# Four tiles of an output projection computed as two pairs of seven block products instead of eight

## The reference, cut to what matters

```python
m = sigmoid(proj[..., o5:o6]) * y_a + sigmoid(proj[..., o6:]) * y_b
x = x + gate * (m @ w_out[l])          # the output projection
...
return rms_norm(x, g_final), ...       # mean square over the 1024 channels of a token
```

## Time and profile before

| | |
|---|---|
| median of 3 runs | 940.15 us (938.82 to 940.74) |
| the profiled execution | 938.97 us, span of the trace 937.2 us |
| PE busy | 916.6 us, 98% of the span |
| DVE / ACT / POOL busy | 736.6 / 385.9 / 88.7 us |
| block products (26 pairs and 8 small ones) | from about 85 to 640.6 us of the span |
| output projection, tiles 1 to 5 | 844 to 901 us |

### The profile page before, as it was taken

One profiled execution on the slowest core, in us unless ns is written; L12 is line 12 of the kernel. 1 busy time (PEld: TensorE's weight loads), 2 busy tenths in 40 slices (PEclk: granted clock), 3 DMA queues, 4 the chain that ended last, 5 costly groups with the idle time before them and its releaser, 6 DMA issues.

```text
span 937.2 us, 16711 instructions
## 1 busy us (share of the span) xinstructions
PE 916.6 (98%) x6928; PEld 897.4 (96%) x6928; DVE 736.6 (79%) x862; ACT 385.9 (41%) x540; POOL 88.7 (9%) x97
## 2 busy tenths in 40 slices
PE   8999999999999999999999999999999999999996
PEld 5699999999999999999999999999999999999996
DVE  1797999997999996989995899999897642443346
ACT  5483355434453443453443454345535311112342
POOL 0121211111021011111010310000000000000000
PEclk9999999999999999999999999999999999999999
DMA  9978998889688989798798985449851524142105
GB/s 368 337 192 216 217 230 230 239 254 235 163 218 243 263 235 243 192 234 245 251 244 251 227 198 154 140 139 322 363 227 46 221 117 157 45 170 102 45 1 181
DMA packets 77741, 191.14 MB, mean 204 GB/s; under 512 B 11617, under 2 KB 18145, under 8 KB 73697
## 3 DMA queue, kind: packets, MB, share of 16 engines
q1 hardware_dynamic: 48176, 119.54, 36.5%
q0 software_dynamic: 19328, 46.17, 24.8%
q10 hardware_dynamic: 10160, 24.35, 7.3%
HBM read 164.07 MB, written 80.49 MB: 261 GB/s over the span
## 4 chain that ended last, share of the span: by engine, by line
PE 65%; DVE 26%; DMA 3%; issue 3%; ACT 1%; SPq 1%; DVEq 0%; ACTq 0%
DVE conv_y L1635 12%; PE ps L844 11%; PE ps L847 11%; PE ps L845 10%; PE ps L907 10%; PE ps L913 10%; PE ps L909 10%; DVE hr L1514 4%; DMA ada_raw<-w_ada 2%; DVE pool_s L1594 1%; DMA raw<-w_sums 1%; DVE bf L1708 1%; DVE stage_hi L1714 1%; DVE sig L1599 1%; DVE pool_p L1611 1%
## 5 line engine op out<-in xcount | busy, mean ns | idle before, releaser
L1635 DVE SCALAR_TENSOR_TENSOR conv_y<-conv_u,par_all,conv_y 128x1024 f32<-128x1024 f32 x240 | 300.6, 1278 | 2.1 <-DVE conv_y L1621 0.6
L907 PE MATMUL ps<-tr,hr 128*128 128x258 f32 x824 | 215.8, 283 | 5.2 <-DVEq L1582 3.4
L909 PE MATMUL ps<-tr,hr 128*128 128x258 f32 x824 | 216.3, 283 | 0.0
L1209 ACT ACTIVATE hr<-raw 128x512 fp32r<-128x512 f32 (+1 forms) x188 | 116.1, 619 | 140.0 <-PE ps L913 66.9
L913 PE MATMUL ps<-tr,hr 128*128 128x258 f32 x824 | 166.3, 283 | 0.0
L907 PEld LDWEIGHTS ps<-tr,hr 128*128 128x128 f32 x824 | 156.8, 190 | 6.1 <-issue 4.1
L907 PE MATMUL ps<-hr 128*128 128x258 f32 x616 | 160.9, 282 | 1.0 <-DVE pool_u L1539 1.0
L909 PE MATMUL ps<-hr 128*128 128x258 f32 x616 | 161.5, 283 | 0.0
L909 PEld LDWEIGHTS ps<-tr,hr 128*128 128x128 f32 x824 | 155.7, 189 | 0.0
L1514 DVE TENSOR_TENSOR hr<-raw,hr 128x512 fp32r<-128x512 f32 (+1 forms) x188 | 126.0, 673 | 8.1 <-ACT hr L1209 4.0
L913 PEld LDWEIGHTS ps<-tr,hr 128*128 128x128 f32 x824 | 127.2, 188 | 0.0
(11 more groups left out here) (200 smaller groups left out, 1276.2 us busy)
## 6 DMA issues: line engine op xcount, KB each, us to landing
w_sums<-w_main POOLq DMA_DIRECT2D x56, 512.0 KB, 9.0
raw<-w_sums SPq DMA_DIRECT2D x104, 256.0 KB, 4.0
raw<-w_main SPq DMA_DIRECT2D x82, 256.0 KB, 4.6
w_sums<-w_sums POOLq DMA_DIRECT2D x26, 512.0 KB, 5.6
w_raw<-w_main SPq DMA_DIRECT2D x24, 512.0 KB, 4.5
w_sums<-w_main ACTq DMA_DIRECT2D x22, 512.0 KB, 5.2
ada_raw<-w_ada SPq DMA_DIRECT2D x8, 1024.0 KB, 20.8
bf<-x_t SPq DMA_DIRECT2D x4, 1032.0 KB, 8.3
```

The lines of the kernel that those rows point to most:

```text
L907: nc.tensor.matmul(bank[:, c, :], wh[:, w_cols], x_hi[:, k, t_cols], start=start and k == 0, stop=False, skip_group_check=True)
L909: nc.tensor.matmul(bank[:, c, :], wh[:, w_cols], x_lo[:, k, t_cols], start=False, stop=False, skip_group_check=True)
L1209: nc.scalar.activation(ring(q)[0][:, 0:n], raw4[:, q % 4, 0:n], ACT.Copy).then_inc(item_hi, 1)
L1635: ins = v.scalar_tensor_tensor(out=y, in0=conv_u[:, x, k:k + SEQ], scalar=par_all[:, g, x, k:k + 1], in1=y, op0=ALU.mult, op1=ALU.add)
```

## The change

Tiles 0 and 1 of the output projection stay plain, tiles 2 and 3 and tiles 4 and 5 become two pairs (A and B) of seven block products, and tiles 6 and 7 stay chunk by chunk, now 7 ahead of 6. The four sums of blocks of m are made by DVE from the full rows of m, split by ACT and DVE, and lie in the rows that held a (the hidden rows of the convolution branch, `zone_h` and `zone_b`). The 14 weight blocks pass through a ring in `w_raw`, `w_hi` and `w_lo`. A fourteenth round of weight sums is added on POOL. x is no longer loaded at once into eight rows: it is loaded tile by tile into two rows (`x_res`), each load behind the tile that frees the row. In the diff `...` stands for what is left out.

```diff
...
+OUT_A, OUT_B = N, N + 1
+OUT_TILE = {OUT_A: 2, OUT_B: 4}
+OUT_ITEMS = [("P1", OUT_A), ("P1", OUT_B), ("P6", OUT_A), ("P2", OUT_A), ("P7", OUT_A), ("P5", OUT_A), ("P4", OUT_A), ("P3", OUT_A),
+             ("P6", OUT_B), ("P2", OUT_B), ("P7", OUT_B), ("P5", OUT_B), ("P4", OUT_B), ("P3", OUT_B)]
+OUT_AT = {item: i for i, item in enumerate(OUT_ITEMS)}
+FIRST_STRASSEN = JOB_OUT + 2
...
-MEAN_AT = {3 * 9 + 1: 0, 3 * 9 + 2: 1, 3 * 12 + 1: 2, 3 * 12 + 2: 3}
+MEAN_AT = {3 * 9 + 1: 0, 3 * 9 + 2: 1, 3 * 12 + 1: 2, 3 * 12 + 2: 3, 3 * 13 + 1: 4, 3 * 13 + 2: 5}
...
+        out_tr = [at("out_tr_h", [2, 2, KH, HALF], F32R, zone_h), at("out_tr_b", [2, 2, KH, HALF], F32R, zone_b)]
+        out_tf = [at("out_tf_h", [2, 2, KH, HALF], F32, zone_h), at("out_tf_b", [2, 2, KH, HALF], F32, zone_b)]
+        u2_out, u3_out = row_mean[:, 0:HALF], row_mean[:, HALF:TOK]
+        sq_tile = pool_s1[:, 0:TOK]
...
+        def x_res(m):
+            return stage_lo[:, m % 2, :] if m < KT - 2 else hf[:, m - (KT - 2), :]
...
+            if q >= OUT_SPLIT:
+                s, half = raw_slot(q) // 2, raw_slot(q) % 2
+                cols_ = slice(half * FORM_COLS, (half + 1) * FORM_COLS)
+                return w_hi[:, s, cols_], w_lo[:, s, cols_]
...
+            def load_out_item(i):
+                form, n = OUT_ITEMS[i]
+                if i < 4:
+                    sp.wait_ge(w_lo_done, lo_count(JOB_OUT + i // 2))
+                else:
+                    sp.wait_ge(item_lo, OUT_SPLIT + i - 3)
...
+            load_x(0)
+            load_x(1)
+            for i in range(4):
+                load_out_item(i)
+            sp.wait_ge(x_new_ready, 1)
+            load_x(2)
+            sp.wait_ge(x_new_ready, 2)
+            load_x(3)
+            for i in range(4, len(OUT_ITEMS)):
+                load_out_item(i)
+            sp.wait_ge(x_new_ready, 3)
+            load_x(5)
+            sp.wait_ge(x_new_ready, 4)
+            load_x(4)
+            sp.wait_ge(item_lo, OUT_SPLIT + 12)
+            sp.dma_start(w_raw[:, 1, :], t["w_main"][MAIN_B + JOBS - 1 - JOB_B]).then_inc(raw_full[1], 16)
+            sp.wait_ge(item_done, LAST + OUT_AT["P6", OUT_B] + 1)
+            load_x(6)
+            load_x(7)
+            sp.wait_ge(item_lo, OUT_SPLIT + 14)
+            sp.dma_start(w_raw[:, 0, :], t["w_main"][MAIN_B + JOBS - 2 - JOB_B]).then_inc(raw_full[0], 16)
...
+            for step in range(3 * SUM_CHUNKS + 3):
                 c, k = step // 3, step % 3
                 if c >= 1:
                     sum_phase(c - 1, 3 + k)
-                if c < N // 2:
+                if c < SUM_CHUNKS:
                     sum_phase(c, k)
                 if step in MEAN_AT:
                     add_row(MEAN_AT[step])
-            for r in range(4, 6):
-                add_row(r)
...
-            job_pairs(JOB_OUT + 1, 4, m_hi, m_lo)
-            single(JOB_OUT + 5, m_hi, m_lo)
+            single(JOB_OUT + 1, m_hi, m_lo)
+            def out_t_product(i, bank, form, n, start=False):
+                if n == OUT_A:
+                    pe.wait_ge(t_lo_done, 4 + OUT_T_LO.index(form) + 1)
+                block_product(OUT_SPLIT + i, bank, out_t(form, 0), out_t(form, 1), start=start).then_inc(item_done, 1)
+            for i, (form, n) in enumerate(OUT_ITEMS):
+                pe.wait_ge(item_lo, OUT_SPLIT + i + 1)
+                if form == "P1":
+                    pe.wait_ge(dve_evac, FIRST_STRASSEN - 1 + (n - OUT_A) - JOB_B)
+                    block_product(OUT_SPLIT + i, bank_a(n), gr[:, 0:KH, HALVES[0]], gr[:, KT:KT + KH, HALVES[0]], start=True).then_inc(item_done, 1)
+                if form == "P2":
+                    pe.wait_ge(seeded, n + 1)
+                    block_product(OUT_SPLIT + i, bank_b, gr[:, KH:KT, HALVES[0]], gr[:, KT + KH:2 * KT, HALVES[0]]).then_inc(item_done, 1)
+                if form == "P3":
+                    pe.wait_ge(c22_out, n + 1)
+                    block_product(OUT_SPLIT + i, bank_c, gr[:, KH:KT, HALVES[1]], gr[:, KT + KH:2 * KT, HALVES[1]]).then_inc(item_done, 1)
+                if form == "P6":
+                    pe.wait_ge(seeded, n + 1)
+                    out_t_product(i, bank_a(n), form, n)
+                if form == "P7":
+                    pe.wait_ge(u2_ready, n + 1)
+                    out_t_product(i, bank_a(n), form, n)
+                if form == "P4":
+                    pe.wait_ge(u3_ready, n + 1)
+                    out_t_product(i, bank_a(n), form, n)
+                if form == "P5":
+                    pe.wait_ge(c12_out, n)
+                    out_t_product(i, bank_c, form, n, start=True)
...
+                    if c == 0 and s == JOBS - 1 and k == 0:
+                        pe.wait_ge(w_lo_done, lo_count(FIRST_STRASSEN))
+                        pe.wait_ge(c21_out, OUT_B + 1)
+                        pe.wait_ge(c11_out, OUT_B + 1)
+                    if c == 0 and s == JOBS - 2 and k in (0, KH):
+                        pe.wait_ge(w_lo_done, lo_count(FIRST_STRASSEN + 1 + k // KH))
...
+            out_t_hi("P5", 1)
+            out_t_hi("P7", 2)
+            item_split(OUT_SPLIT)
+            item_split(OUT_SPLIT + 1)
+            out_t_hi("P6", 3)
+            out_t_hi("P4", 4)
+            tile_square(0, 0)
+            item_split(OUT_SPLIT + 2)
+            item_split(OUT_SPLIT + 3)
+            out_seed(OUT_A)
+            tile_square(1, 1)
+            for i, (form, n) in enumerate(OUT_ITEMS):
+                act.wait_ge(item_done, LAST + i + 1)
+                if form == "P6":
+                    if n == OUT_B:
+                        act.wait_ge(c12_out, n)
+                    nc.scalar.activation(halves(u2_out), bank_a(n), ACT.Copy).then_inc(u2_ready, 1)
+                if form == "P7":
+                    if n == OUT_B:
+                        act.wait_ge(c22_out, n)
+                    nc.scalar.activation(halves(u3_out), bank_a(n), ACT.Copy).then_inc(u3_ready, 1)
+                if (form, n) == ("P2", OUT_A):
+                    out_seed(OUT_B)
+                if i + 4 < len(OUT_ITEMS):
+                    item_split(OUT_SPLIT + i + 4)
...
+            def out_result(i):
+                form, n = OUT_ITEMS[i]
+                m = OUT_TILE[n]
+                landed = 16 * (m // 2 + 1)
+                first, second = HALVES
+                if form not in ("P2", "P5", "P4", "P3"):
+                    return
+                dve.wait_ge(item_done, LAST + i + 1)
+                if form == "P2":
+                    dve.wait_ge(xres_loaded[0], landed)
+                    v.scalar_tensor_tensor(out=halves(hf[:, KT + m, first]), in0=bank_b, scalar=mod[:, 4 + m // 4, m % 4, 0:1],
+                                           in1=halves(x_res(m)[:, first]), op0=ALU.mult, op1=ALU.add).then_inc(c11_out, 1)
+                if form == "P5":
+                    dve.wait_ge(u3_ready, n + 1)
+                    v.scalar_tensor_tensor(out=halves(hf[:, KT + m + 1, second]), in0=bank_c, scalar=-1.0, in1=halves(u3_out),
+                                           op0=ALU.mult, op1=ALU.subtract).then_inc(c22_out, 1)
+                    dve.wait_ge(c22_out, n + 1)
+                    dve.wait_ge(xres_loaded[1], landed)
+                    second_half(m + 1)
+                if form == "P4":
+                    link(v.scalar_tensor_tensor(out=halves(hf[:, KT + m + 1, first]), in0=bank_a(n),
+                                                scalar=minus_gate[:, (m + 1) // 4, (m + 1) % 4:(m + 1) % 4 + 1],
+                                                in1=halves(x_res(m + 1)[:, first]), op0=ALU.mult, op1=ALU.add))
+                    dve.sem_inc(c21_out, 1)
+                    dve.sem_inc(x_new_ready, 1)
...
+                if form == "P3":
+                    dve.wait_ge(u2_ready, n + 1)
+                    v.tensor_tensor(halves(hf[:, KT + m, second]), bank_c, halves(u2_out), ALU.add).then_inc(c12_out, 1)
+                    dve.wait_ge(c12_out, n + 1)
+                    second_half(m)
+                    dve.sem_inc(x_new_ready, 1)
...
+            plain_x(0)
+            item_lo_part(OUT_SPLIT)
+            item_lo_part(OUT_SPLIT + 1)
+            link(v.scalar_tensor_tensor(out=ot2, in0=ot1, scalar=-1.0, in1=m_rows[:, KH:KT, HALVES[1]], op0=ALU.mult, op1=ALU.subtract))
+            dve.sem_inc(t_summed, 1)
+            link(v.scalar_tensor_tensor(out=ot4, in0=ot2, scalar=-1.0, in1=m_rows[:, KH:KT, HALVES[0]], op0=ALU.mult, op1=ALU.subtract))
+            dve.sem_inc(t_summed, 1)
+            out_t_lo("P6", 3)
+            plain_x(1)
+            item_lo_part(OUT_SPLIT + 2)
+            item_lo_part(OUT_SPLIT + 3)
+            out_t_lo("P7", 2)
+            out_t_lo("P5", 1)
+            add_square(1)
+            for i in range(len(OUT_ITEMS)):
+                out_result(i)
+                if i + 4 < len(OUT_ITEMS):
+                    item_lo_part(OUT_SPLIT + i + 4)
+                if i == 0:
+                    out_t_lo("P4", 4)
...
```

(9 more changed lines are left out.)

192 lines of the change are left out of this document (137 added, 55 removed).

## The result

The changed kernel takes 934.96 us (median of 5 runs, 933.97 to 936.02), the kernel before 940.03 us (5 runs, 938.82 to 940.74): a ratio of 0.995, with an interval of 0.9935 to 0.9964. That is 5.1 us less by the medians, and 3.4 to 6.1 by the interval; 935.0 was forecast. The profiled execution took 934.96 us, with a span of 933.2.

What follows compares the result with a forecast made beforehand. PE, busy 98% of the span, was taken to bound the kernel: 45.4 us of matmuls removed, 40.4 added, 5.1 less, the first projection at 0, so 940.15 - 5.1 = 935.0 us; range 933.2 to 938.4.

Steps and rivals of the forecast that it cites:

- PE's part: Tiles 2 to 5: 288 plain matmuls (45.4 us) give way to 336 shorter ones (40.4 us), 5.1 us less.
- a part that doesn't shrink with its columns: Price of a matmul on PE: from 344 to 258 columns it falls to 76%, not 75%.
- The seams: Waits of PE between the 14 items: 0.03 us an item in the first projection, so 0.5 us.
- The front of the items: Fifth to seventh item: DVE and ACT have operands ready with 1.6, 1.7 and 1.4 us to spare.
- Loads: Fifth item's weight block, behind x of tile 3: issued at 858.1, lands in 4.8 us, by 862.9.
- The end: Last tiles, 7 and 6: the end moves with PE, -5.1 us; the norm's sums have 0.9 us of room.
- The first projection: One more round of weight sums and two row sums there cost 0; upper end 1.5 us.
- the stage up to 855 us: Everything before the items stays in place; tile 1 ending later than 856.5 would show the prediction wrong.
- Rival 2: Fifth item waits for memory; gain gone if its block lands at 871.0, then one for one; 945 at 18 us; chance 0.04.
- the forecast's upper end: Upper end of the forecast case for the whole kernel, 934.0 to 936.2 us, chance 0.63.

Runs made afterwards that it cites:

- the kernel with eight products: The changed kernel with P1 of each pair multiplied twice into the same banks, so eight block products per pair for seven: 941.45 us, ratio 1.0001.
- the three runs with additions: The changed kernel with two, three or four more row additions on DVE ahead of the low part of the fifth item's weights: 936.26, 938.27, 940.74 us.
- the round alone: The kernel before with only the fourteenth round of weight sums and the two row sums moved in among it, all output tiles plain: 939.80 us.

## Why the prediction was right

- *PE's part.* 45.4 us removed, 40.4 added, 5.1 less. The trace after has 40.41 us, and the kernel with eight products 46.19 us. Both prices were measured in the kernel before in long stretches without a wait, and that made this term exact. The whole time is not known as well: its interval, 3.4 to 6.1 us, holds the 5.1. What the prediction said of the price ("a part that doesn't shrink with its columns") was a sound reading of two points and no more: the third point, 0.112 us at 128 and 130 columns, and the 0.10 at 9 lie far above its line.
- *The seams.* 0.5 us was allowed by the first projection's waits and none was seen.
- *The front of the items.* 1.6, 1.7 and 1.4 us of room were worked out, 1.6, 1.7 and 1.5 are in the trace, and the three runs with additions give 1.5. DVE's 32 us in that stretch (80%) were 29.7 (73%); the prediction's prices are distances of starts, with waits in them that are not busy time, as 4.2 us for three rows of squares where 3.7 were busy. The prediction didn't name `u2` as a place; it had 2.1 us of room.
- *Loads.* The fifth block was taken to be there by 862.9, worked out for a tile 1 that ended 0.9 us earlier. ACT took it up at 863.23, having waited for it, so it landed 0.5 us earlier than forecast by that clock.
- *The end.* It moved with PE, and its room was 0.9 us, as worked out.
- *The first projection.* Taken at 0, and the round alone measured 0.9989 of the time, with 1 in the interval. That the stage up to 855 us stays where it is didn't hold to the letter: tile 1 ended at 856.54, past the 856.5 that the prediction had set as its limit. Whether the change moved it is open (the last point below).
- *What was off.* Rival 2 and the forecast's upper end priced a wait of PE at its own length. A wait of 0.8 us cost about 1 us, one of 2.1 us cost about 1.7 more than itself, one of 3.4 us about 2.7 more, and one of 4.9 about 2 more, since the clock went to half behind them in these profiles. As an estimate, from the ratios 0.9981 and 1.0009 at 2.1 and 3.4 us, the gain is gone with a wait of about 3 us, not 5.1.
- *What stays open.* The 0.7 us that the profile after lost at the load of the convolution's output. PE's wait there was 1.6 to 1.8 us in ten profiles (of the changed kernel and nine of its variants) and 0.9 in the two others; it was 0.9 in the kernel before and with the sums alone. The end of tile 1 doesn't follow it: 855.53 us in a variant with the long wait, 857.01 in one with the short. It could be chance, or a cost of the changed program. The medians (5.07 us measured, 5.1 from PE's items alone) do without such a cost, but with an interval of 3.4 to 6.1 us they can't exclude 0.7 us either. Open as well is when the clock falls behind a wait.

## What to carry to other kernels

Where PE works without a gap, what a rewrite of its products is worth is a product of counts and distances of starts, and both distances can often be read in the kernel before, if it uses the form elsewhere. Seven products for eight save one eighth of the columns but pay in shorter matmuls: here 258 columns in place of 344 kept 89% of that gain (5.1 of 5.7 us), and a second level with 129 columns would lose by far: as an estimate, seven eighths of 672 matmuls at 0.1116 us are 65.6 us, against 40.4. The rest of the work is to show that the engines that prepare the first items keep ahead by a known margin, and that margin has to be followed through every engine's list in order: a late load reached PE through an unrelated copy behind it in ACT's list. A wait of PE of 1.8 us or more can cost 1.5 to 2.8 us beyond its length, when the clock falls to half behind it; it did so 12 times out of 19 here.
